# Hybrid encoder step on one core: the low halves of the output projection move from GpSimd to VectorE

## What is computed

```python
a = attend(q, k, v) @ w_attn_out                       # (T, 512) @ (512, 1024)
c = silu(layernorm(c)) @ w_conv_out + b_conv_out       # (T, 512) @ (512, 1024)
x = x + (sigmoid(g_attn) * a + sigmoid(g_conv) * c) @ w_out
up, new_ffn = causal_dwconv(rmsnorm(x, norm2_g) @ w_up, ...)
gate, val = split(up); x = x + (silu(gate) * val) @ w_down
```

## Time and profile before

| what | value |
|---|---|
| runs | 1724.4, 1726.33, 1728.26 us |
| the profiled execution | 1728.74 us, of which the span of its instructions is 1726.9 us |
| TensorE busy | 1682.7 us, 97% of the span, 9642 matmuls |
| VectorE busy | 1136.2 us, 66%, 1644 instructions |
| ScalarE busy | 615.5 us, 36% |
| GpSimd busy | 126.7 us, 7%, 82 instructions |
| output projection | about 707 to 888 us of the span |
| second norm | about 888 to 928 us |

### The profile page before, as it was taken

The page is one execution under the profiler, slowest core; times in us unless marked ns, Lnnn a source line. Parts: engine busy times, 40 slices in busy tenths (PEclk is TensorE's granted clock), DMA queues, the critical chain, the costliest instruction groups (busy, mean ns, idle before and its releaser), DMA issues. The chain is left out here.

```text
span 1726.9 us, 26412 instructions
## 1 busy us (share of the span) xinstructions
PE 1682.7 (97%) x9642; PEld 1562.7 (90%) x9642; DVE 1136.2 (66%) x1644; ACT 615.5 (36%) x1549; POOL 126.7 (7%) x82
## 2 busy tenths in 40 slices
PE   6899999999999999999999999999999999999998
PEld 6889888898898999989989999999999999999996
DVE  5469889799896225345458676656766567665677
ACT  6435646456445234211135221312213122231324
POOL 3200000000000113233221000000000000000000
PEclk9999999999999999999999999999999999999999
DMA  6230230500412522632221120201102021120102
GB/s 195 73 82 1 78 89 2 142 26 13 138 51 63 182 88 89 212 109 81 88 76 61 49 62 25 61 21 52 61 24 61 12 61 50 35 61 12 61 13 106
DMA packets 145878, 119.40 MB, mean 69 GB/s; under 512 B 6763, under 2 KB 130127, under 8 KB 145800
## 3 DMA queue, kind: packets, MB, share of 16 engines
q1 hardware_dynamic: 145800, 118.35, 22.4%
HBM read 95.83 MB, written 22.50 MB: 69 GB/s over the span
## 5 line engine op out<-in xcount | busy, mean ns | idle before, releaser
L1520 PE MATMUL bank<-h2hi,whi 128*128 128x364 f32 (+1 forms) x1056 | 347.6, 329 | 2.1 <-PEq L1526 2.1
L1520 PE MATMUL bank<-h2lo,whi 128*128 128x364 f32 (+1 forms) x1056 | 347.6, 329 | 0.0
L1520 PE MATMUL bank<-h2hi,wlo 128*128 128x364 f32 (+1 forms) x1056 | 347.5, 329 | 0.0
L1305 DVE TENSOR_TENSOR x<-bank,x 128x512 f32<-128x512 f32 x270 | 181.0, 688 | 166.6 <-PE bank L1295 161.8
L1520 PEld LDWEIGHTS bank<-h2hi,whi 128*128 128x128 f32 x1056 | 199.0, 188 | 2.7 <-issue 2.3
L1520 PEld LDWEIGHTS bank<-h2lo,whi 128*128 128x128 f32 x1056 | 199.0, 188 | 0.4
L1520 PEld LDWEIGHTS bank<-h2hi,wlo 128*128 128x128 f32 x1056 | 199.0, 188 | 0.0
L732 DVE SCALAR_TENSOR_TENSOR c_sb<-u,dww,c_sb 128x1118 f32<-128x1118 f32 x120 | 165.4, 1379 | 1.3
L1295 PE MATMUL bank<-whi,mhi 128*128 128x512 f32 x342 | 134.4, 393 | 4.4 <-DVE x L1305 3.2
L1295 PE MATMUL bank<-whi,mlo 128*128 128x512 f32 x342 | 134.1, 392 | 0.0
L1295 PE MATMUL bank<-wlo,mhi 128*128 128x512 f32 x342 | 134.0, 392 | 0.0
(11 more groups left out here) (193 smaller groups left out, 3525.2 us busy)
## 6 DMA issues: line engine op xcount, KB each, us to landing
wraw<-in_w_up SPq DMA_DIRECT2D x88, 256.0 KB, 3.2
wraw<-in_w_in SPq DMA_DIRECT2D x30, 512.0 KB, 5.2
wraw<-in_w_down SPq DMA_DIRECT2D x44, 256.0 KB, 2.7
scr_gate<-gst SPq DMA_DIRECT2D x11, 544.0 KB, 4.3
gch<-scr_gate SPq DMA_DIRECT2D x16, 364.0 KB, 3.7
xt<-in_x_prompt SPq DMA_DIRECT2D x8, 512.0 KB, 5.0
kpast<-in_cache_sb_k SPq DMA_DIRECT2D x16, 256.0 KB, 6.4
vpast<-in_cache_sb_v SPq DMA_DIRECT2D x16, 256.0 KB, 5.3
```

The costliest lines, as they stand in the source:

```text
L1305: dve.tensor_tensor(y, bank[banks[d % len(banks)]][:, :], y, ALU.add).then_inc(down_ev, 1)
L1520: mm = pe.matmul(bank[(3 * tau + c) % 4][:, 0:c1_ - c0], w[:, ws], x[:, k, c0:c1_], start=(k == 0 and n == 0), stop=(k == KT - 1 and n == 2))
```

## The change

GpSimd's programs in both blocks are gone, and VectorE does their subtractions. Six `mix_lo` stand one place behind the six mixes of a round; four `weight_lo4` stand behind the adds 3 and 7 and at the end of the 18 adds; in the second norm four `first_lo` stand at the end of the tiles 2, 4 and 6 and behind the last `h2lo`. Nothing else changes; the semaphores keep their counts.

```diff
-            @block.gpsimd
-            def _(pool):
-                def round_(i, slots):
...
-                            pool.wait_ge(m_hi_done, 6 * i + 3 * j + c + 1)
-                            pool.tensor_tensor(mlo[:, j, c0:c1_], mixa[:, (3 * j + c) % 2, 0:c1_ - c0],
-                                               mhi[:, j, c0:c1_].bitcast(F32), ALU.subtract).then_inc(m_lo_done, 1)
-                    for k, slot in enumerate(slots):
-                        make_lo(pool, raw4, 4 * i + k, k % 2, wlo[:, slot, :], whi[:, slot, :])
...
+                def mix_lo(i, j, c):
+                    c0, c1_ = CHUNKS[c]
+                    dve.wait_ge(m_hi_done, 6 * i + 3 * j + c + 1)
+                    dve.tensor_tensor(mlo[:, j, c0:c1_], mixa[:, (3 * j + c) % 2, 0:c1_ - c0],
+                                      mhi[:, j, c0:c1_].bitcast(F32), ALU.subtract).then_inc(m_lo_done, 1)
+
+                def weight_lo4(i, k):
+                    make_lo(dve, raw4, 4 * i + k, k % 2, wlo[:, 1 + k, :], whi[:, 1 + k, :])
+
                 def round_(i):
-                    for j in range(2):
-                        for c in range(3):
-                            mix(i, j, c)
+                    for n in range(7):
+                        if n < 6:
+                            mix(i, n // 3, n % 3)
+                        if n:
+                            mix_lo(i, (n - 1) // 3, (n - 1) % 3)
 
                 def down_adds(i):
                     for d in range(18):
                         down_add(dve, d, i, dn4_ready, dn4_ev)
+                        if d in (3, 7):
+                            weight_lo4(i, d // 4)
+                    for k in (2, 3):
+                        weight_lo4(i, k)
...
-                @block.gpsimd
-                def _(pool):
-                    for k, (slot, _what) in enumerate(FIRST_FFN):
-                        make_lo(pool, raw4, 4 * LAST + k, k % 2, wlo[:, slot, :], whi[:, slot, :])
...
+                    def first_lo(k):
+                        slot = FIRST_FFN[k][0]
+                        make_lo(dve, raw4, 4 * LAST + k, k % 2, wlo[:, slot, :], whi[:, slot, :])
...
                         if t:
                             lo_parts5(t - 1)
+                        if t in (2, 4, 6):
+                            first_lo(t // 2 - 1)
                     lo_parts5(NT - 1)
+                    first_lo(3)
```

More of the change, by code:

```diff
@@ L1368, in _ @@
                 round_(NI - 1, True)
-            @block.gpsimd
-            def _(pool):
-                def round_(i, slots):
-                    for j in range(2):
-                        for c, (c0, c1_) in enumerate(CHUNKS):
-                            pool.wait_ge(m_hi_done, 6 * i + 3 * j + c + 1)
-                            pool.tensor_tensor(mlo[:, j, c0:c1_], mixa[:, (3 * j + c) % 2, 0:c1_ - c0],
-                                               mhi[:, j, c0:c1_].bitcast(F32), ALU.subtract).then_inc(m_lo_done, 1)
-                    for k, slot in enumerate(slots):
-                        make_lo(pool, raw4, 4 * i + k, k % 2, wlo[:, slot, :], whi[:, slot, :])
-                with pool.Fori(0, NI - 1) as i:
-                    round_(i, (1, 2, 3, 4))
-                round_(NI - 1, ())
             @block.scalar
@@ L1436, in mix @@
                     dve.tensor_tensor(mixa[:, x, 0:n], mixa[:, x, 0:n], mixc[:, x, 0:n], ALU.add).then_inc(mix_done, 1)
-                def round_(i):
-                    for j in range(2):
-                        for c in range(3):
-                            mix(i, j, c)
+                def mix_lo(i, j, c):
[5 more added lines that the diff above has]
+                    make_lo(dve, raw4, 4 * i + k, k % 2, wlo[:, 1 + k, :], whi[:, 1 + k, :])
+                def round_(i):
+                    for n in range(7):
[3 more added lines that the diff above has]
+                            mix_lo(i, (n - 1) // 3, (n - 1) % 3)
                 def down_adds(i):
```

## The result

The changed kernel takes 1733.89 us in the median of 14 runs (1728.94 to 1735.68), the kernel before beside it 1727.22 us (1723.1 to 1730.09): a ratio of 1.0039 with a 95% interval of 1.0030 to 1.0047, or 5.2 to 8.1 us more. The profiled execution took 1732.74 us, its span 1731.0.

A forecast was written before the change was run, and what follows sets the result against it. TensorE was taken to bound the rounds, VectorE narrowly the second norm's tiles and its end. Terms 1.15 + 2.28 + 1.14 = +4.57 us on the 1726.33 us median gave 1730.9 us, range 1727.5 to 1734.3.

The forecast's parts named there:

- What bounds the kernel: TensorE bounds the rounds with VectorE half idle; the second norm is tight on both, VectorE setting the pace by a hair.
- the three places named: Where TensorE waits for VectorE: end of round 0, the second norm's tiles, and the second norm's end.
- Round 0, +1.15: At the end of round 0, two mix subtractions delay the first add and down job 4 by 1.15 us.
- The sign that it named: In round 0 of the changed profile, TensorE's wait before down job 4 would be near 3.3 us.
- The tiles, +2.28: In the second norm, two weight subtractions ahead of tiles 3 and 5 cost 2 x 1.14 us; the third is hidden.
- the end, +1.14: At the second norm's end, the fourth weight subtraction behind the last `h2lo` adds 1.14 us.
- the tiles absorb it: In the second norm, TensorE sets the tile pace and VectorE's slack takes two subtractions: 2.3 us slower, 1728.6; chance 0.22.
- GpSimd's absence, 0: At round starts and tile 7, 4.2 us of VectorE time come free, none where TensorE waits: 0.
- the rival's 4.2 us: At round starts and tile 7, instructions GpSimd held up are on the path; 4.2 us come off, 1726.7; chance 0.07.
- SyncE's queue, 0: Round 1's gates, queued behind slab 3, go out at about 752, not 747.04, still in time: cost nothing.
- The clock, 0: Behind TensorE's two longer pauses, the lower granted clock adds 0, between -1.1 and one or two low stretches at 1.7.
- a rival of 0.12: Longer pauses in tiles 3 and 5, round 0 and the end bring another low-clock stretch costing 1.7 us: 1732.6; chance 0.12.

The follow-up runs named there:

- the projection alone: Against the kernel before, only the output projection's subtractions moved to VectorE, the second norm's four staying on GpSimd: 1727.44 us, ratio 1.0011.
- the second norm alone: Against the kernel before, only the second norm's four weight subtractions moved to VectorE, the projection keeping GpSimd: 1729.11 us, ratio 1.0021.
- the version with the three terms removed: Changed kernel with mixes reordered, first two second-norm subtractions in the gain wait, fourth in the last-transposes wait: 1726.60 us, 1.0001 of before.
- the two filled kernels: Changed kernel with 16 unread matmuls in TensorE's pause behind the last transposes, and kernel before with 9: 1730.93 and 1725.33 us.

## Why the prediction was right, and where its size was off

*What bounds the kernel:* right. The cost lay in the three places named; rounds 1 to 3 cost nothing, with 29.23 us of VectorE work in a stretch of 48 and TensorE busy 48.00 of 48 us in round 1 and 49.00 of 49 in round 2. But "There are three" left out a fourth place: in the trace of before TensorE's down job 6, at the start of the second norm, already waited 1.04 us for VectorE:

```profile
892.72 0.47 PE L1295 MATMUL bank<-whi,mhi 128*128 128x512 f32 x1 [1.04 <-DVE x L1305]
```

*Round 0, +1.15:* 1.10 in the trace; 1.9 (0.3 to 3.5) with the projection alone, which also holds the longer transfer of the gain. The sign that it named, a wait near 3.3 us before down job 4, did not come (2.15). Its condition, that the gates' landing cancels in the difference, can hold on average only: the last mix starts anywhere between 735.13 and 737.92 in the fourteen profiles, and the profile that the prediction was read from is the latest of them.

*The tiles, +2.28, and the end, +1.14:* 2 x 1.14 and 1.14 in the trace; 3.6 us (2.1 to 5.2) with the second norm alone. That the third subtraction would be hidden and the other two not was right, and with it the answer to the rival "the tiles absorb it": VectorE had no slack there.

*GpSimd's absence, 0:* right, within what the runs can tell. The instructions that it held up became short, as the rows of lines 1436 and 1421 show, and the version with the three terms removed is no faster than before (ratio 0.9990 to 1.0012), so the rival's 4.2 us did not come. The Trainium skill's section "Who interferes with whom" on the page "SBUF — State Buffer" says that a VectorE instruction with two SBUF inputs contends with a GpSimd instruction that reads SBUF; the rows agree (up to 1778 ns beside GpSimd, at most 540 without). They tell which instructions grow, and here no wait of TensorE stood behind the grown ones.

*SyncE's queue, 0:* right. The gates of round 1 were sent 3.5 us later than before (750.55 for 747.04), where some 5 had been reckoned, and the first mix of round 1 followed the weights without a wait.

*The gain's transfer:* not in the sum at all, since the fourth place was not in the count. The transfer there became 0.5 us longer (the mean of 4.0 us against 3.6), and TensorE's pause behind it, where VectorE still waits for the gain first, grew with it: from between 1.43 and 1.75 us to between 1.96 and 2.22. One profile against one could not have told this from scatter.

*The clock, 0:* this is the term that was mis-sized, by the estimate that follows. The prediction said "I take 0, between -1.1 and one or two more stretches at 1.7", and put the further stretches into a rival of 0.12 with 1732.6 us. The mean clock fell from 0.9961 to 0.9954 on one chip, and was 0.9951 in the first 14 runs: 0.0007 to 0.0010 of the span, or 1.2 to 1.7 us (the last set of seven runs each shows no fall). All 25 runs of the changed kernel against all 97 of the kernel before with a clock on record, on partly different chips, give 0.0009 (0.0002 to 0.0016 by their scatter). The measured time is inside the range because its upper end had room for two more low stretches; the point forecast had none. The step that failed was to reckon the clock from one profile, in which both pauses of before happened to be followed by a low stretch, as if they always were. In the profiles at hand the pause of 2.35 us at the end (from the start of the last transpose to the start of the next matmul, the kernel before and versions with that pause) was followed by a low stretch in 2 of 5, the longer one of 3.48 us in 6 of 6, twice for nearly 7 us, and the filled one of under 1 us in none of 3. In round 0, by the same measure, the pauses of 2.40 to 2.86 us had one in 5 of 5, those from 0.80 to 2.15 us in 0 of 9, and that pause is what the change lengthens by 1.1 us: of the seven profiles with the change's order of the mixes four have a low stretch there, of the seven with the first add right behind the mix one. And in the second profile of the changed kernel, of mean clock 0.991, the pause before down job 6, at 2.22 us the longest of nine between 1.96 and 2.22, was followed by one too, with 0.50 in its middle row:

```profile
894.00:896.00 2.00, 2.00 (x8) 1.65 (x9) 1.96 (x4) 0.00 (x0) 0.00 (x0) 0.86 0.00 0
896.00:898.00 2.00, 2.00 (x7) 1.41 (x6) 0.41 (x1) 0.00 (x0) 0.00 (x0) 0.50 0.00 0
898.00:900.00 2.00, 2.00 (x13) 1.86 (x12) 1.74 (x3) 0.52 (x2) 0.00 (x0) 0.79 0.00 0
```

So in these profiles a longer pause costs its length and also makes the low stretch likelier.

*What stays open.* 4.5 us of the forecast's waits, 0.5 of the gain's transfer and 1.2 to 1.7 of clock make 6.2 to 6.7, within both intervals of the change (5.2 to 8.1 and 3.6 to 7.4); the first two, 5.0, are also near what lies between the two filled kernels (5.4 in the means). But the clock's share is a mean over few runs with a coarse clock, the second norm alone drew hardly any of it, and the pause in round 0 was not filled by itself. So the waits are shown; that the changed kernel runs at a lower mean clock shows in the pooled runs; what that costs, and at which of the pauses, is an estimate.

## What to carry to other kernels

Work moved to a half-idle engine costs nothing where that engine idles and its full pitch where it sets the pace, so read its waits stage by stage: here 35 of 40 moved subtractions left no pause of TensorE, and five (two in round 0, one each before tiles 3 and 5, one at the end) decided the time. Before adding an instruction to an engine that closes a block or feeds a waiting engine, look for a wait on a transfer or on another engine and put it there: the three shifts took the loss back. Ask of each pause of TensorE not only how long it is but whether the low clock behind it becomes likelier, and from more than one profile.

## What the runs showed of the hardware that was not expected

One and the same pause of TensorE can go either way: behind that of 2.35 us at the end of the second norm the granted clock fell in 2 of 5 profiles. Filling it with matmuls that compute nothing of use brought 2.1 us in the medians of the kernel before (its interval still holds zero), and the mean clock from 0.9960 to 0.9968. The transfer of 512 KB at the start of the second norm took 0.5 us longer after a change that left it and its queue as they were. And the landing of the gates in round 0 scatters by 2.2 us between six profiles of kernels that are alike up to there (the last mix starts between 735.13 and 737.31), which is more than most terms of this sum; a single pair of profiles would have shown no difference in TensorE's wait in round 0 at all.
